# Masked copies of the 128x128 inverses: from VectorE to GpSimd from the third level on

## The chip, the cores and the metric

The kernel runs on one core of a Trainium2 chip. The metric is the device time of one launch in microseconds (us); lower is better. A core has TensorE (PE in the views, with its weight loads as PEld), VectorE (DVE), ScalarE (ACT), GpSimd (POOL), and SyncE (SP), which here only starts transfers. Each engine works through its own instructions in the order in which they are written, and engines meet only at semaphores.

## The reference, cut to what matters

The program is two transformer-like blocks, one after the other, over 1024 tokens of width 1024. The change sits in the gated delta rule of the second block. Per head and chunk of tokens it solves a unit lower triangular system, and then a short recurrence runs over the chunks:

```python
m_low = jnp.where(strict, jnp.einsum('nbhid,nbhjd->nbhij', kb, kc) * decay, 0.0)
lhs = m_low + jnp.eye(CHUNK, dtype=jnp.float32)
sol = lax.linalg.triangular_solve(lhs, rhs, left_side=True, lower=True, unit_diagonal=True)
u, w = sol[..., :dv], sol[..., dv:]
...
v_new = u_i - jnp.einsum('bhcd,bhde->bhce', w_i, S)
o = jnp.einsum('bhcd,bhde->bhce', qd_i, S) + jnp.einsum('bhij,bhje->bhie', attn_i, v_new)
S = S * gl_i[..., None, None] + jnp.einsum('bhcd,bhce->bhde', kd_i, v_new)
```

The kernel uses chunks of 128 tokens in place of 64, which gives the same output, and computes the inverse of `lhs` instead of solving. The inverse is built by doubling: if the inverses of the diagonal blocks of size s are known, those of size 2s follow from the part of the matrix that lies between two neighbouring blocks. With 128 rows there are seven levels, 0 to 6.

## The kernel before, in words

There are 4 heads and 8 chunks, so 32 matrices of 128x128. Four of them (two chunks, two heads) lie side by side in one tile of 128x512 and are worked on as one group, so there are 8 groups, b = 0 to 7. Four lanes share them: lane 0 does groups 0 and 2, lane 1 does 4 and 6, lane 2 does 1 and 3, lane 3 does 5 and 7 (`LANES`). A lane has four work tiles (`WB[n]`), all called wb in the views: `Mm` (the matrix), `Tm`, `Yy` and `Ml` (its masked copy). The running inverse of a group is in `Z`.

Each engine has a generator per lane (`prep_pe`, `prep_act`, `prep_dve`), and each `yield` ends a step. One group takes 16 steps: four of preparation, and then two for each level l = 1 to 6. `delta_steps` runs the same numbered steps s = 0 to 50 on TensorE, ScalarE and VectorE. In a step it takes the lanes in the order 0, 1, 2, 3; lane n starts at s = 4n; from s = 20 on a piece of the recurrence over the chunks (`chunk_pe` and its like) follows the lanes. So lane 0 has its first group at s = 0 to 15 and its second at s = 16 to 31, lane 1 has them four steps later, lane 2 eight and lane 3 twelve.

The work of a level l of one group:

- First step of the level. TensorE multiplies with the masked copy (L2959, four products of 128x128, "the y product" below, semaphore kind `pp_y`), and for l > 1 transposes `Z` (L2964). ScalarE copies both results from PSUM (L2992, L2996). VectorE, once the y product has read `Ml`, writes the masked copy for the next level into it (`lmask(l + 1)`, L3035, kind `pp_l`); it has one `Ml` per lane.
- Second step of the level. TensorE multiplies again (L2971), and VectorE subtracts the result from `Z` (L3056, kind `pp_z`), which the next level's y product needs.

The masked copy is `Ml = Mm * lev[l]`, 128x512 numbers, with a 0/1 mask of 128x128 repeated four times. Copies for levels 0 and 1 are made during the preparation.

The preparation has a product of decays (L2929, named bg), from which VectorE makes two tiles (L3015, L3017); ScalarE takes exponentials of them (L2979, L2982, L2985); TensorE multiplies keys with keys and queries (L2942, L2945), and VectorE scales (L3023).

What sets the order is only the order in which the code is written, engine by engine, and the waits. A wait is for a count of a semaphore that several kinds share: all of TensorE's signals of this stage (`prep_pe` in the order listings) count in TensorE's order. GpSimd does nothing in this stage; its last work lies some 1400 us earlier.

Of the kernel before, what the change touches and what calls it, by code (L numbers as in the profile page):

```python
# [195 lines left out]
class Signals:  # L196
# [18 lines left out]
    def give(self, kind, *which):  # L215
        return self.count(kind, which, 1)
# [112 lines left out]
def build(nc, A, out, scr, spill, bsc):  # L329
    from contextlib import ExitStack  # L330
    ctx = ExitStack()
    with ctx:
        sig = Signals(lambda kind: ctx.enter_context(nc.semaphore(kind)))
        give, land = sig.give, sig.land
# [449 lines left out]
        def s5_pool(pool):  # L784
            pool.wait_ge("xn_lo", 7)
            pool.wait_ge("bsc")
            pool.e.memset(Mk, 0.0).then_inc(*give("s5_mzero"))
# [1101 lines left out]
        def sb_pool(pool):  # L1889


            def mask(t, ds, *signal):
                pool.e.affine_select(out=t[:, ds], in_=t[:, ds], pattern=[[1, 128]], compare_op=ALU.is_gt,
                                     fill=0.0, base=0, channel_multiplier=-1).then_inc(*give(*signal))

            for h in range(4):
                units = SBU[h]
                n = len(units)
                for i in range(n + 3):
                    if i < n and units[i]["ds"]:  # L1900
                        u = units[i]
                        pool.wait_ge("sb_sp", u["n"])
                        mask(sbwk[u["n"] % 5][1], u["ds"], "sb_masked", u["n"])
                    if 0 <= i - 2 < n and units[i - 2]["ds"]:
                        u = units[i - 2]
                        pool.wait_ge("sb_w", u["n"])
                        mask(sbwk[u["n"] % 5][0], u["ds"], "sb_y", u["n"])
# [162 lines left out]
        FH, FSG, _, FUV = ffn_tiles(y_at + TB, False)  # L2070
# [283 lines left out]
        lev = mem("lev", y_at + 9728, [128, 896])  # L2354
# [564 lines left out]
        v3 = lambda z: z.rearrange("p (n c) -> p n c", n=4)  # L2919
        i3 = ident.unsqueeze(1).to_broadcast([128, 4, 128])  # L2920

        def prep_pe(pe, ring, b, wb):
            Mm, Tm, Yy, Ml = wb
            Zb = Z[:, b, :]
            yield
            ps = bank.take(pe, ring, f"bg{b}", ("pp_ex", b))
            pe.wait_ge("pp_lb", b)
            for n in range(4):
                ins = pe.e.matmul(ps[:, sl[n]], Ml[:, sl[n]], upper, start=True, stop=True)  # L2929
            ins.then_inc(*give("pp_bg", b))  # L2930
            yield
            ba = bank.take(pe, ring, f"ba{b}", ("pp_m", b))
            bq = bank.take(pe, ring, f"bq{b}", ("pp_at", b))
            for n, (c, h) in enumerate(PREP[b]):
                cc = slice(128 * c, 128 * c + 128)
                kx, qx = FT[h][1], FT[h][0]
                pe.wait_ge("unit", 4 + h)
                pe.wait_ge("unit", h)
                if h < 2:
                    pe.wait_ge(f"lane{2 * h}", "unpark")  # L2940
                    pe.wait_ge(f"lane{2 * h + 1}", "unpark")
                ka = pe.e.matmul(ba[:, sl[n]], kx[:, cc], kx[:, cc], start=True, stop=True)  # L2942
                if n == 3:
                    ka.then_inc(*give("pp_a", b))
                kq = pe.e.matmul(bq[:, sl[n]], kx[:, cc], qx[:, cc], start=True, stop=True)  # L2945
            kq.then_inc(*give("pp_q", b))
            yield
            ps = bank.take(pe, ring, f"bt{b}", ("pp_z", b, 0))
            pe.wait_ge("pp_l", b, 0)
            for n in range(4):  # L2950
                ins = pe.e.transpose(ps[:, sl[n]], Ml[:, sl[n]], ident)
            ins.then_inc(*give("pp_t", b))
            yield
            for l in range(1, 7):
                ps = bank.take(pe, ring, f"b1{b}{l}", ("pp_ye", b, l))
                pe.wait_ge("pp_l", b, l)
                pe.wait_ge("pp_z", b, l - 1)
                for n in range(4):
                    ins = pe.e.matmul(ps[:, sl[n]], Ml[:, sl[n]], Zb[:, sl[n]], start=True, stop=True)  # L2959
                ins.then_inc(*give("pp_y", b, l))  # L2960
                if l > 1:
                    ps = bank.take(pe, ring, f"b3{b}{l}", ("pp_tm", b, l))
                    for n in range(4):
                        ins = pe.e.transpose(ps[:, sl[n]], Zb[:, sl[n]], ident)  # L2964
                    ins.then_inc(*give("pp_zT", b, l))
                yield
                ps = bank.take(pe, ring, f"b2{b}{l}", ("pp_z", b, l))
                pe.wait_ge("pp_ye", b, l)
                pe.wait_ge("pp_tm", b, l) if l > 1 else pe.wait_ge("pp_t1", b)
                for n in range(4):  # L2970
                    ins = pe.e.matmul(ps[:, sl[n]], Tm[:, sl[n]], Yy[:, sl[n]], start=True, stop=True)  # L2971
                ins.then_inc(*give("pp_tx", b, l))
                yield
# [26 lines left out]
        def prep_dve(dve, b, wb, before):  # L3000
            Mm, Tm, Yy, Ml = wb
            Zb, ATb = Z[:, b, :], AT[:, b, :]
            if before is None:
                dve.wait_ge("prod", O0 - 1)
            else:
                dve.wait_ge("pp_tx", before, 6)
            dve.wait_ge("la")
            for n, (c, h) in enumerate(PREP[b]):
                ins = dve.e.tensor_scalar(Ml[:, sl[n]], ones, la[:, c, h:h + 1], None, ALU.mult)
                ins.then_inc(*(give("pp_lb", b) if n == 3 else dve.step()))  # L3010
            yield
            bg = bank.of(f"bg{b}")
            dve.wait_ge("pp_bg", b)
            dve.wait_ge("c_mS")
            dve.e.scalar_tensor_tensor(v3(Tm), v3(bg), -1.0, mS.unsqueeze(1).to_broadcast([128, 4, 128]), ALU.mult, ALU.add).then_inc(*give("pp_d", b, 0))  # L3015
            dve.wait_ge("c_mT")
            dve.e.tensor_tensor(v3(Yy), v3(bg), mT.unsqueeze(1).to_broadcast([128, 4, 128]), ALU.add).then_inc(*give("pp_d", b, 1))  # L3017
            yield
            ba, bq = bank.of(f"ba{b}"), bank.of(f"bq{b}")
            for n, (c, h) in enumerate(PREP[b]):  # L3020
                dve.wait_ge("pp_a", b)
                dve.wait_ge("pp_e1", b, 3)
                ins = dve.e.scalar_tensor_tensor(Mm[:, sl[n]], ba[:, sl[n]], beta[:, c, h:h + 1], Tm[:, sl[n]], ALU.mult, ALU.mult)  # L3023
                ins.then_inc(*(give("pp_m", b) if n == 3 else dve.step()))
            dve.wait_ge("pp_q", b)
            dve.wait_ge("pp_e2", b, 3)
            dve.e.tensor_tensor(ATb, bq, Yy, ALU.mult).then_inc(*give("pp_at", b))
            for n, (c, h) in enumerate(PREP[b]):
                qx = FT[h][0][:, 128 * c:128 * c + 128]
                dve.wait_ge("pp_ex", b)  # L3030
                dve.e.tensor_tensor(qx, qx, Ml[:, sl[n]], ALU.mult).then_inc(*dve.step())

            def lmask(l):
                m = lev[:, 128 * l:128 * l + 128].unsqueeze(1).to_broadcast([128, 4, 128])
                dve.e.tensor_tensor(v3(Ml), v3(Mm), m, ALU.mult).then_inc(*give("pp_l", b, l))  # L3035

            dve.wait_ge(*dve.last)
            dve.wait_ge("pp_m", b)
            dve.wait_ge("c_lev")
            lmask(0)  # L3040
            yield
            dve.wait_ge("pp_l", b, 0)
            dve.e.scalar_tensor_tensor(v3(Tm), v3(Ml), -1.0, i3, ALU.mult, ALU.add).then_inc(*give("pp_t1", b))
            dve.wait_ge("pp_t", b)
            dve.e.scalar_tensor_tensor(v3(Zb), v3(bank.of(f"bt{b}")), -1.0, i3, ALU.mult, ALU.add).then_inc(*give("pp_z", b, 0))
            dve.wait_ge("pp_t1", b)
            lmask(1)
            yield
            for l in range(1, 7):
                if l < 6:  # L3050
                    dve.wait_ge("pp_y", b, l)
                    lmask(l + 1)
                yield
                dve.wait_ge("pp_tx", b, l)
                dve.wait_ge("pp_z", b, l - 1)
                dve.e.tensor_tensor(Zb, Zb, bank.of(f"b2{b}{l}"), ALU.subtract).then_inc(*give("pp_z", b, l))  # L3056
                yield

# [73 lines left out]
        def lane_of(prep, eng, n, *ring):  # L3134
            for b in LANES[n]:
                yield from prep(eng, *ring, b, WB[n])
# [362 lines left out]
        def gpsimd(pool):  # L3499
            s5_pool(pool)  # L3500
            sb_pool(pool)

        def sync(sp):
            input_sp(sp)
# [100 lines left out]
```

## Time and profile before

| | us |
|---|---|
| median of 3 runs | 3736.06 |
| lowest and highest | 3735.85, 3736.31 |
| the profiled execution: its own time | 3736.58 |
| the profiled execution: span of the trace | 3735.0 |
| TensorE busy | 3535.2 |
| VectorE busy | 1655.9 |
| ScalarE busy | 1167.6 |
| GpSimd busy | 25.1 |

Busy times come from the first part of the page. The stage of the change lies between 2626 and 2832 us of the span, a little over 5% of it. A matmul's busy time overlaps that of its neighbour, so the pitch at which groups of matmuls start says more than the sum: a y product (four products in eight records) starts 0.89 us after the one before when nothing waits.

### The profile page before, as it was taken

The page shows a single profiled execution, that of the slowest core. Times are in us where ns is not written, and L with a number is a line of the kernel's source. Part 1 is how long each engine was busy: PE and PEld are TensorE (multiplying, and loading weights), DVE is VectorE, ACT ScalarE, POOL GpSimd, SP SyncE. Part 2 cuts the span into 40 slices and gives each one's busy share as a digit, 9 for nine tenths or more (in the row PEclk, how much of TensorE's full clock was granted, in tenths as well). Part 3 has the DMA queues.
Part 4 walks back from the last instruction along what each step waited for, and adds up shares of the span by engine and source line. Part 5 has one row for each costly group of instructions (what it writes and reads, how often), then busy time and mean ns, then how long its engine had stood idle before and what let it go on. Part 6 is the DMA issues. An engine that isn't in the chain of part 4 may idle for free.

```text
span 3735.0 us, 38804 instructions
## 1 busy us (share of the span) xinstructions
PE 3535.2 (95%) x16598; PEld 2863.6 (77%) x16598; DVE 1655.9 (44%) x2033; ACT 1167.6 (31%) x1610; POOL 25.1 (1%) x69
## 2 busy tenths in 40 slices
PE   7999999998999899999999979999899899999997
PEld 5778887777766688888888858787797588888785
DVE  7444452224554344333233364444764453534354
ACT  3232213333255623111111145344343521212122
POOL 0000000000000000000000000000000000000000
PEclk9999999999999999999999989999999999999998
DMA  2213241112400121111111112121112011111111
GB/s 107 58 48 127 82 170 44 45 50 94 138 29 23 39 86 68 44 53 46 57 35 62 39 44 85 62 90 62 46 46 101 18 50 53 47 55 38 54 35 56
DMA packets 80971, 232.11 MB, mean 62 GB/s; under 512 B 12296, under 2 KB 22280, under 8 KB 80784
## 3 DMA queue, kind: packets, MB, share of 16 engines
q1 hardware_dynamic: 80800, 229.64, 18.5%
q8 instruction: 131, 2.15, 0.2%
q14 instruction: 40, 0.33, 0.0%
HBM read 201.04 MB, written 27.38 MB: 61 GB/s over the span
## 4 chain that ended last, share of the span: by engine, by line
PE 83%; DVE 8%; ACT 7%; issue 1%; DMA 1%; SPq 0%; ACTq 0%; DVEq 0%
PE PS L431 71%; PE PS L443 2%; PE PS L2959 1%; PE PS L2971 1%; PE PS L1757 1%; PE PS L1466 1%; ACT dS L1520 1%; PE PS L858 1%; PE PS L449 1%; PE PS L1779 1%; DVE xlo L465 1%; DVE dO L1584 0%; PE PS L2964 0%; DVE wlo L396 0%; ACT whi L391 0%
## 5 line engine op out<-in xcount | busy, mean ns | idle before, releaser
L431 PE MATMUL PS<-xhi,whi 128*128 128x512 f32 x3120 | 996.4, 401 | 52.3 <-DVE xlo L465 37.0
L431 PE MATMUL PS<-xlo,whi 128*128 128x512 f32 x3120 | 969.9, 392 | 0.0
L431 PE MATMUL PS<-xhi,wlo 128*128 128x512 f32 x3120 | 967.3, 391 | 0.0
L431 PEld LDWEIGHTS PS<-xhi,whi 128*128 128x128 f32 x3120 | 583.5, 190 | 198.0 <-issue 49.8
L431 PEld LDWEIGHTS PS<-xlo,whi 128*128 128x128 f32 x3120 | 590.6, 189 | 125.8
L431 PEld LDWEIGHTS PS<-xhi,wlo 128*128 128x128 f32 x3120 | 590.3, 189 | 125.5
L396 DVE TENSOR_TENSOR wlo<-raw,whi 128x1024 fp32r<-128x1024 f32 (+3 forms) x307 | 329.6, 1075 | 504.3 <-ACT whi L391 504.2
L391 ACT CAST whi<-raw 128x1024 fp32r<-128x1024 f32 (+3 forms) x307 | 284.2, 926 | 505.3 <-PE PS L431 484.8
L431 PE MATMUL PS<-fhi,whi 128*128 128x512 f32 x704 | 218.5, 392 | 8.5 <-DVE flo L465 8.5
L431 PE MATMUL PS<-flo,whi 128*128 128x512 f32 x704 | 217.9, 391 | 0.0
L431 PE MATMUL PS<-fhi,wlo 128*128 128x512 f32 x704 | 217.8, 391 | 0.0
L431 PEld LDWEIGHTS PS<-fhi,whi 128*128 128x128 f32 x704 | 132.6, 189 | 37.6 <-DVE flo L465 10.2
L431 PEld LDWEIGHTS PS<-fhi,wlo 128*128 128x128 f32 x704 | 133.0, 189 | 27.8
L431 PEld LDWEIGHTS PS<-flo,whi 128*128 128x128 f32 x704 | 132.9, 189 | 27.7
L462 ACT CAST fhi<-fuv 128x1024 fp32r<-128x1024 f32 x44 | 46.1, 1049 | 328.5 <-DVE fuv L2149 221.9
L431 PE MATMUL PS<-yhi,whi 128*128 128x512 f32 x352 | 111.4, 398 | 8.2 <-DVE ylo L465 8.2
L431 PE MATMUL PS<-ylo,whi 128*128 128x512 f32 x352 | 110.3, 395 | 0.0
L431 PE MATMUL PS<-yhi,wlo 128*128 128x512 f32 x352 | 110.2, 395 | 0.0
L2216 DVE TENSOR_SCALAR fcb<-fsg,V 128x1024 f32<-128x1024 f32 x44 | 35.7, 812 | 163.9 <-ACT fsg L2192 163.9
L2232 DVE SCALAR_TENSOR_TENSOR merged<-PS,mod,merged 128x1024 f32<-128x1024 f32 x32 | 41.1, 1284 | 149.9 <-PE PS L431 149.9
L2156 DVE TENSOR_TENSOR merged<-PS,merged 128x1024 f32<-128x1024 f32 x32 | 39.2, 1224 | 137.8 <-PE PS L431 137.8
L2192 ACT COPY fsg<-PS 128x1024 f32<-128x1024 f32 x44 | 44.6, 1015 | 174.3 <-PE PS L431 174.3
(473 smaller groups left out, 3656.2 us busy)
## 6 DMA issues: line engine op xcount, KB each, us to landing
raw<-in_w_up SPq DMA_DIRECT2D x88, 512.0 KB, 3.3
raw<-in_w_in SPq DMA_DIRECT2D x67, 512.0 KB, 3.3
adr<-in_w_ada SPq DMA_DIRECT2D x48, 512.0 KB, 4.5
raw<-in_w_gate SPq DMA_DIRECT2D x32, 512.0 KB, 3.4
raw<-in_w_down SPq DMA_DIRECT2D x32, 384.0 KB, 3.1
raw<-in_w_down SPq DMA_DIRECT2D x32, 320.0 KB, 2.9
raw<-in_w_br SPq DMA_DIRECT2D x24, 256.0 KB, 2.7
x<-in_xT SPq DMA_DIRECT2D x8, 512.0 KB, 8.3
```

The source lines that it names most:

```text
L391: act.e.copy(whis[i % RING][:, 0:kt, :], raws[i % RING][:, 0:kt, :]).then_inc(*give("w_hi", i))
L396: dve.e.tensor_tensor(wlos[i % RING][:, 0:kt, :], raws[i % RING][:, 0:kt, :], whis[i % RING][:, 0:kt, :].bitcast(F32), ALU.subtract).then_ ...
L431: ins = pe.e.matmul(ps[:, h * 512:(h + 1) * 512], w[s][:, k, :], x[:, h * 512:(h + 1) * 512], start=(at == 0 and n == 0), stop=(at == kt - ...
L443: ins = pe.e.matmul(ps[:, h * 512:(h + 1) * 512], ones, x[:, h * 512:(h + 1) * 512], start=first, stop=last)
L449: ins = pe.e.transpose(ps[:, j * 128:(j + 1) * 128], src[:, j * 128:(j + 1) * 128], ident)
L462: act.e.copy(dst, src).then_inc(*give(*signal))
L465: dve.e.tensor_tensor(dst, src, hi.bitcast(F32), ALU.subtract).then_inc(*give(*signal))
L858: ins = pe.e.matmul(o, H[m][rows, n, :], CL[m][rows, i, 1:9, :].rearrange("p a b -> p (a b)"), start=False, stop=(m == 1), skip_group_chec ...
L1466: ins = pe.e.matmul(ps[:, 64 * h:64 * h + 64], dP[u % 2][:, n, k, :], Vt[:, k0 // 128 + k, 64 * h:64 * h + 64], start=(k == 0), stop=(k == ...
L2156: dve.e.tensor_tensor(X2[:, ft, :], psum.of(j), X2[:, ft, :], ALU.add).then_inc(*give("f1_x", c, ft))
L2192: act.e.copy(GSG[v][:, FPAD:], psum.of(j)).then_inc(*give("f2_raw", v, i))
L2232: dve.e.scalar_tensor_tensor(X1[:, ft, :], psum.of(j), gt_f(ft), X1[:, ft, :], ALU.mult, ALU.add).then_inc(*give("f2_x", c, ft))
```

## The change

The masked copies for levels 2 to 6 leave VectorE (`lmask(l + 1)` for l = 1 to 5) and are made on GpSimd by a new generator, `prep_pool`. They get a semaphore of their own, `pp_lp`, and the y product waits for that one from level 2 on. GpSimd's instruction waits for the same two things: the y product of level l, and `pp_z` of level 0.

GpSimd does not run under `delta_steps` but under a loop of its own, `delta_pool`, of the same shape. A group takes 14 of its steps and not 16: four of preparation and two for each of l = 1 to 5.

```diff
             for l in range(1, 7):
                 ps = bank.take(pe, ring, f"b1{b}{l}", ("pp_ye", b, l))
-                pe.wait_ge("pp_l", b, l)
+                pe.wait_ge("pp_l", b, l) if l < 2 else pe.wait_ge("pp_lp", b, l)
                 pe.wait_ge("pp_z", b, l - 1)
...
             for l in range(1, 7):
-                if l < 6:
-                    dve.wait_ge("pp_y", b, l)
-                    lmask(l + 1)
                 yield
...
+        def prep_pool(pool, b, wb):
+
+            Mm, Tm, Yy, Ml = wb
+            for _ in range(4):
+                yield
+            for l in range(1, 6):
+                pool.wait_ge("pp_y", b, l)
+                pool.wait_ge("pp_z", b, 0)
+                m = lev[:, 128 * (l + 1):128 * (l + 1) + 128].unsqueeze(1).to_broadcast([128, 4, 128])
+                pool.e.tensor_tensor(v3(Ml), v3(Mm), m, ALU.mult).then_inc(*give("pp_lp", b, l + 1))
+                yield
+                yield
+
+        def delta_pool(pool):
+            pool.wait_ge("c_lev")
+            lanes = [lane_of(prep_pool, pool, n) for n in range(4)]
+            for s in range(44):
+                for n in range(4):
+                    if s >= 4 * n:
+                        next(lanes[n], None)
...
         def gpsimd(pool):
             s5_pool(pool)
             sb_pool(pool)
+            delta_pool(pool)
```

The `Ml` tiles of lanes 0, 1, 2 and 3 are wb_325, wb_329, wb_333 and wb_337 in the listings below.

TensorE at its steps s = 19 and 20, of the kernel before: the second group of lane 0 has its first y product, lanes 2 and 3 are still in their first groups.

```order
5801 L2971 MATMUL PS<-wb_336,wb_335 128x128 [waits prep_act]
5803 L2959 MATMUL PS<-Z_320,wb_325 128x128 [waits prep_dve]
5805 L2959 MATMUL PS<-Z_320,wb_333 128x128 [waits prep_dve]
5807 L2964 MATMUL PS<-ident_50,Z_320 128x128 x4
5808 L2959 MATMUL PS<-Z_320,wb_337 128x128 [waits prep_dve]
5810 L2964 MATMUL PS<-ident_50,Z_320 128x128 [waits prep_act]
5812 L2971 MATMUL PS<-wb_324,wb_323 128x128 [waits prep_act]
```

The same place in the changed kernel. The order is the same; the y products of lanes 2 and 3 (levels 5 and 3) now wait for GpSimd too.

```order
5801 L2971 MATMUL PS<-wb_336,wb_335 128x128 [waits prep_act]
5803 L2959 MATMUL PS<-Z_320,wb_325 128x128 [waits prep_dve]
5805 L2959 MATMUL PS<-Z_320,wb_333 128x128 [waits prep_dve,pp_lp]
5807 L2964 MATMUL PS<-ident_50,Z_320 128x128 x4
5808 L2959 MATMUL PS<-Z_320,wb_337 128x128 [waits pp_lp,prep_dve]
5810 L2964 MATMUL PS<-ident_50,Z_320 128x128 [waits prep_act]
5812 L2971 MATMUL PS<-wb_324,wb_323 128x128 [waits prep_act]
```

GpSimd of the changed kernel around the same place (nothing stands there before). Row 84 is lane 3's copy for level 2, rows 85 to 87 are GpSimd's own step 18, rows 88 to 90 its step 20, rows 91 to 93 its step 22.

```order
84 L3065 TENSOR_TENSOR wb_337<-wb_334,lev_251 128x512 [waits prep_dve,prep_pe]
85 L3065 TENSOR_TENSOR wb_325<-wb_322,lev_251 128x512 [waits prep_dve,prep_pe]
86 L3065 TENSOR_TENSOR wb_333<-wb_330,lev_251 128x512
87 L3065 TENSOR_TENSOR wb_337<-wb_334,lev_251 128x512
88 L3065 TENSOR_TENSOR wb_325<-wb_322,lev_251 128x512 [waits prep_pe]
89 L3065 TENSOR_TENSOR wb_333<-wb_330,lev_251 128x512
90 L3065 TENSOR_TENSOR wb_337<-wb_334,lev_251 128x512
91 L3065 TENSOR_TENSOR wb_325<-wb_322,lev_251 128x512 [waits prep_pe]
92 L3065 TENSOR_TENSOR wb_329<-wb_326,lev_251 128x512 [waits prep_dve,prep_pe]
93 L3065 TENSOR_TENSOR wb_337<-wb_334,lev_251 128x512
```

Row 85 waits for the y product of TensorE's row 5803, and rows 86 and 87, which are the copies that rows 5805 and 5808 wait for, stand behind it.

## Rows read from the trace of the kernel before

**Rows 1.** The page's part 1: busy time and share of each engine.
```profile
PE 3535.2 (95%) x16598; PEld 2863.6 (77%) x16598; DVE 1655.9 (44%) x2033; ACT 1167.6 (31%) x1610; POOL 25.1 (1%) x69
```

**Rows 2.** TensorE's waits, 2626 to 2832 us: waiter, releaser, us, times, longest.
```profile
PE PS L2951 <- DVE wb L3035: 5.8, 3, 4.9
PE PS L2959 <- DVE Z L3056: 4.9, 5, 1.7
PE PS L2942 <- ACT wb L2996: 4.3, 2, 2.7
PE PS L2959 <- ACT wb L2992: 4.0, 2, 2.1
```

**Rows 3.** Groups by line and shape, 2626 to 2832: count, busy us, mean ns.
```profile
L3035 DVE TENSOR_TENSOR wb<-wb,lev 128x512 f32<-128x512 f32 x56 | 37.8, 688 | 25.4 <-PE PS L2959 24.9
```

**Rows 4.** Timelines of TensorE and VectorE at step 9, then VectorE's waits, same stretch.
```profile
2651.10 1.06 PE L2929 MATMUL PS<-upper,wb 128*128 128x128 f32 x8
...
2652.42 0.69 DVE L3015 SCALAR_TENSOR_TENSOR wb<-PS,mS 128x512 f32<-128x512 f32 x1
...
DVE wb L3015 <- PE PS L2929: 1.0, 5, 0.2
```

**Rows 5.** Timelines of TensorE and VectorE at step 20: start, us, engine, line.
```profile
2706.14 1.95 PE L2959 MATMUL PS<-Z,wb 128*128 128x128 f32 x16
...
2708.37 1.06 PE L2959 MATMUL PS<-Z,wb 128*128 128x128 f32 x8
...
2707.24 0.69 DVE L3035 TENSOR_TENSOR wb<-wb,lev 128x512 f32<-128x512 f32 x1 [0.16 <-PE PS L2959]
```

**Rows 6.** The same two timelines at step 22.
```profile
2714.16 1.06 PE L2959 MATMUL PS<-Z,wb 128*128 128x128 f32 x8
...
2717.28 1.06 PE L2959 MATMUL PS<-Z,wb 128*128 128x128 f32 x8
...
2715.26 0.69 DVE L3035 TENSOR_TENSOR wb<-wb,lev 128x512 f32<-128x512 f32 x1 [1.09 <-PE PS L2959]
```

**Rows 7.** The same two timelines at step 24.
```profile
2726.17 1.95 PE L2959 MATMUL PS<-Z,wb 128*128 128x128 f32 x16
...
2727.27 0.69 DVE L3035 TENSOR_TENSOR wb<-wb,lev 128x512 f32<-128x512 f32 x1 [0.16 <-PE PS L2959]
```

**Rows 8.** The same two timelines at step 26.
```profile
2740.93 1.06 PE L2959 MATMUL PS<-Z,wb 128*128 128x128 f32 x8
...
2737.08 0.69 DVE L3035 TENSOR_TENSOR wb<-wb,lev 128x512 f32<-128x512 f32 x1 [0.64 <-PE PS L2959]
```

**Rows 9.** GpSimd: line L1893 (ns min/median/max), its groups, one timeline row.
```profile
L1893 POOL TENSOR_SCALAR_AFFINE_SELECT sbt<-sbt x64: 285/292/550, 1009.4 to 1247.9; 128x128 f32<-128x128 f32 x64
...
L787 POOL MEMSET Mk<- 128x4096 f32 x1 | 3.5, 3531 | 70.1 <-DMA bsc<-brow 70.1
L3595 POOL MEMSET const-bfloat16-1.0<- 128x1 bf16 x1 | 0.1, 101 | 0.0
...
1143.89 0.55 POOL L1893 TENSOR_SCALAR_AFFINE_SELECT sbt<-sbt 128x128 f32<-128x128 f32 x1 [3.85 <-DVE sbt L1914]
```

**Rows 10.** TensorE's timeline where it waited long: the wait stands in brackets.
```profile
2657.76 0.46 PE L2942 MATMUL PS<-FT 128*128 128x128 f32 x2 [2.71 <-ACT wb L2996]
...
2677.85 1.16 PE L2959 MATMUL PS<-Z,wb 128*128 128x128 f32 x8 [2.14 <-ACT wb L2992]
...
2761.69 1.16 PE L2959 MATMUL PS<-Z,wb 128*128 128x128 f32 x8 [1.91 <-ACT wb L2992]
```

**Rows 11.** Stretches: length, then busy us (records) of PE, PEld, DVE, ACT, POOL; then PEclk.
```profile
2658.60:2661.60 3.00, 3.00 (x16) 3.00 (x16) 1.11 (x5) 0.00 (x0) 0.00 (x0) 0.50 0.00 0
2679.00:2682.00 3.00, 3.00 (x17) 3.00 (x15) 0.69 (x1) 1.32 (x3) 0.00 (x0) 0.50 0.00 0
...
2739.40:2742.40 3.00, 3.00 (x30) 3.00 (x29) 1.50 (x5) 0.88 (x3) 0.00 (x0) 1.00 0.00 0
2761.80:2764.80 3.00, 3.00 (x26) 2.83 (x27) 0.69 (x1) 2.27 (x5) 0.00 (x0) 1.00 0.03 5
```

## The prediction

> **What bounds the kernel now.** I read the page's busy shares first: TensorE is busy 95% of the span, VectorE 44%, GpSimd 1% [rows 1]. So what counts is when TensorE stands still. The second view is the list of TensorE's waits in the stage of the change, 206 us long [rows 2]. There the largest entries are a handful of waits of some us in total each: for VectorE's L3035 (5.8), for VectorE's update of Z (4.9), and for ScalarE's copies (4.3 and 4.0). Together the four are 19.0 us, and this is all that a lighter VectorE could attack. The third view is the timelines of TensorE and VectorE: they say for each of these waits whether a masked copy of level 2 or higher stood ahead of the releaser. The reader is to see that the releaser nearly always started because of TensorE itself, a fraction of a us after the product it needed.
>
> **What leaves VectorE.** 56 masked copies of 688 ns run there now [rows 3]. 40 of them go (8 groups, 5 levels): 27.5 us of VectorE's busy time. They are worth only what TensorE waited behind them. The 5.8 us of L2951 [rows 2] is a wait for the copy of level 0, which stays on VectorE. The two waits for ScalarE follow the exponentials, which start when VectorE has made L3015 and L3017. In 5 of 7 cases L3015 itself waited for TensorE's product L2929 (the last row of [rows 4]), so no copy in front of it held it back. In one of the others, at step 9, L3015 started at 2652.42 without a wait, 1.32 us after its product began at 2651.10 [rows 4]; after the 0.89 us of that product and a hand-over of 0.2 it could have started at 2652.2. That is a gain of **0.2 us**. The waits for Z come behind updates that were themselves released by TensorE, or behind work that stays (copies of keys, weight halves). I take 0.2 us for the whole relief; its upper bound is one copy, 0.69 us, at each of the two preludes not covered by the 5, so 1.4 us, and it can't fall below nothing.
>
> **What GpSimd's order adds.** The copy for level l + 1 is wanted one level later, 9 us or more on, so in most steps GpSimd has time for three copies of a us or two. The exception comes from the 14 steps per group where the other engines have 16. From GpSimd's step 18 on, lane 0's copies for its second group stand two steps too early: each waits for a y product of TensorE's step s + 2, and the copies of lanes still in their first group, which TensorE needs in that very step s + 2, stand behind it. It lasts until all lanes are in their second group, so it touches TensorE's steps 20, 22, 24 and 26. With T for one copy on GpSimd and 0.1 us for the hand-over back to TensorE (the 0.2 of rows 4 at most):
>
> - Step 20. Lane 0's y product starts at 2706.14 and lane 2's at 2706.14 + 0.89 = 2707.03 [rows 5]. VectorE could start its copy behind lane 0's product at 2707.24, and so can GpSimd. It makes two copies before lane 2 may go on: 2707.24 + 2T + 0.1 against 2707.03, a wait of 2T + 0.31.
> - Step 22. Lane 0's product is seen at 2715.26, lane 2 wants to start at 2717.28, since lane 1's preparation lies between [rows 6]: 2T - 1.92.
> - Step 24. Here lane 1's first product of its second group comes directly before lane 3's: seen at 2727.27, wanted at 2726.17 + 0.89 = 2727.06 [rows 7]: 2T + 0.31.
> - Step 26. Seen at 2737.08, wanted at 2740.93 [rows 8]: 2T - 3.75, which is nothing below T = 1.87.
>
> The third copy in steps 20 and 22 is in time as long as T is under 1.34, the distance 2708.37 - 2707.03 [rows 5]. So the sum is 6T - 1.30 us for T between 0.96 and 1.34. Behind each wait stand the transposes, the third lane's product and the piece of the recurrence, so the whole stage shifts; I find no later wait that would swallow it, because those that follow hang on ScalarE's chain, which starts from TensorE's L2929 and shifts too.
>
> **What T is.** No multiplication on GpSimd is in the trace. Below, it is bounded by the memset: 3531 ns for 4096 columns, 101 ns for one [rows 9], so 0.84 ns a column and 0.53 us for 512, with nothing read. Above, I put twice the cost per column of the mask of 128x128, which reads one operand: (292 - 101)/128 = 1.5 ns a column, twice that for two operands is 3.0, and 1.64 us for 512. Four times the 292 ns gives 1.17 us. I take **1.25 us**: nearest to that row, which reads and writes as the copy does, with a little for the second operand, which is a small mask read four times. That makes 6 x 1.25 - 1.30 = **6.2 us**: 2.8, 0.6 and 2.8.
>
> The Trainium skill, page "GPSIMD Engine Reference", section "Performance versus the Vector engine", gives 4497 ns for an addition of two operands of 2048 columns, which would be 1.12 us for 512, an estimate, and a sum of 5.4 us. No row here shows it.
>
> **What the waits do to the clock.** After waits of 2.71 and 2.14 us TensorE's clock was granted at one half for more than 3 us [rows 10, 11]; after 1.91 us it stayed full. At one half, 16 or 17 records start in 3 us, at full 30 [rows 11]; a stretch of some 3.4 us so costs 1.6 us. The two new waits of 2.8 us are of the kind that brought it, but whether one does hangs on what lies just around it. I take one of the two, **1.6 us**; bounds 0 and 3.2.
>
> **Sum.** -0.2 + 6.2 + 1.6 = +7.6 us. On the profiled execution's own time, 3736.58, that is 3744.2; the median of the runs lies 0.5 lower, so **3743.7 us**. 0.2% of this time is 7.5 us, about what a measurement of this kernel tells from no change; the forecast stands just over it.
>
> **Rivals.**
>
> 1. *No slower stretch of the clock*: the same waits, the clock stays at 2.4 GHz. +6.0, 3742.1 us, which counts as no change. For it: 1.91 us left the clock alone [rows 10, 11]. Against: 2.14 did not. Both waits throttled give +9.2, 3745.3 us.
> 2. *GpSimd is fast (the other side)*: it makes the copy at the memset's pace, T = 0.53. Then only steps 20 and 24 wait, 1.4 us each, too short for the clock: +2.5, 3738.6 us, not slower. It decides below T = 1.0 or so, where sum and clock stay under 5 us. Against it: a mask of a quarter of the size already takes 292 ns [rows 9].
> 3. *Shared access to SBUF*: one of the 64 masks took 0.55 us and not 0.29, right as VectorE read SBUF [rows 9]. If each copy loses time so, and VectorE in turn stands behind copies, T is 2.0: steps 20 and 24 wait 4.3 each, 22 2.1, step 26 0.25, the third lanes 2 x 0.66 more; with both stretches of slow clock +15.3, 3751.4 us. Against it: in steps 20 and 24 VectorE has little left to do. The Trainium skill, page "SBUF — State Buffer", section "Who interferes with whom", says that a VectorE instruction with two SBUF inputs and a GpSimd instruction that reads SBUF exclude each other for their whole length; the 0.55 us agrees, and by that rule most of VectorE's updates of Z, whose second input is in PSUM, would not collide.
> 4. *The relief counts after all*: waits that I put down to TensorE's own chain shrink, because VectorE reaches L3015 and Z earlier everywhere. To end faster by over 0.2% it would have to take 13 of the 19.0 us [rows 2], since GpSimd's order costs 6. I see no place for it.
>
> **How the numbers follow.** The forecast (one slow stretch, T near 1.25) has 0.42, both slow 0.23, none 0.17, rival 2 0.07, rival 3 0.07, rival 4 0.04. The forecast lies on the border, so a good half of it counts as slower: slower 0.24 + 0.23 + 0.06 = 0.53, faster 0.04, no change 0.43. The range for 8 in 10 goes from T = 1.0 with no slow stretch (4.7 - 0.2 = +4.5, 3740.6) to both slow at T = 1.5 (7.7, the third lanes 2 x 0.16, 3.2, less 0.2: +11.0, 3747.1); I widen it by a us or so on each side, towards rivals 2 and 3: 3739.5 to 3748.5.
>
> **What would show it.** In the changed profile: VectorE 27 us less busy, GpSimd with 40 instructions more; TensorE's L2959 waiting for the new GpSimd line three times, about 2.8, 0.6 and 2.8 us, in steps 20, 22 and 24 (near 2707, 2720 and 2732) and almost nowhere else; a mean of 1.2 to 1.3 us for the copy; the clock at one half once more than before between 2700 and 2740. It is wrong if L2959 waits for GpSimd in other steps (then T is far off), if the waits for L3056 or ScalarE shrink by several us (rival 4), or if later waits take up the shift.

## The result and the profile after

| | before | after |
|---|---|---|
| median, us | 3737.12 (12 runs) | 3743.95 (12 runs) |
| lowest and highest, us | 3735.85, 3738.62 | 3742.51, 3747.75 |
| ratio, 95% interval | | 1.0019 [1.001, 1.0028] |
| profiled execution: own time, span, us | 3736.58, 3735.0 | 3747.68, 3746.1 |

The change makes the kernel 6.8 us slower in the medians, where +7.6 (3743.7 us) was forecast. The profiled execution of after is a rather long one: it is 11.1 us longer than that of before. Of these, 4.4 us arose ahead of the stage that was changed, and 1.3 us are won back behind it. All readings below therefore compare distances within the stage.

The page's busy times of the kernel after, as in [rows 1]:

```profile
PE 3539.8 (94%) x16598; PEld 2867.9 (77%) x16598; DVE 1645.0 (44%) x1993; ACT 1168.0 (31%) x1610; POOL 77.2 (2%) x109
```

VectorE has its 40 instructions fewer and GpSimd its 40 more. But VectorE is only 10.9 us less busy, not 27.5. The 16.6 us between are read further down.

TensorE's waits of after in the stage (waiter, releaser, us, times, longest), as in [rows 2]:

```profile
PE PS L2951 <- DVE wb L3035: 5.8, 3, 4.9
PE PS L2959 <- DVE wb L3009: 5.5, 2, 2.8
PE PS L2959 <- DVE Z L3053: 4.9, 5, 1.7
PE PS L2959 <- ACT wb L2992: 4.6, 4, 2.1
PE PS L2942 <- ACT wb L2996: 4.3, 2, 2.7
...
PE PS L2959 <- POOL wb L3065: 0.5, 1, 0.5
```

The entries for L2951, Z and L2942 are what they were. New are 5.5 us "for L3009" and 0.5 us for GpSimd's L3065. L2959 doesn't wait for L3009 in the program, so the name needs the timelines. TensorE's y products of steps 20, 22 and 24, and one of step 12, of after:

```profile
2711.32 1.06 PE L2959 MATMUL PS<-Z,wb 128*128 128x128 f32 x8
2715.05 1.13 PE L2959 MATMUL PS<-Z,wb 128*128 128x128 f32 x8 [2.67 <-DVE wb L3009]
...
2726.03 1.13 PE L2959 MATMUL PS<-Z,wb 128*128 128x128 f32 x8 [0.50 <-POOL wb L3065]
...
2738.84 1.13 PE L2959 MATMUL PS<-Z,wb 128*128 128x128 f32 x8 [2.79 <-DVE wb L3009]
...
2673.53 1.13 PE L2959 MATMUL PS<-Z,wb 128*128 128x128 f32 x8 [0.29 <-ACT wb L2992]
```

And beside them GpSimd's copies and VectorE's L3009 and L3035 (start, length, engine, line, count):

```profile
2712.46 3.71 POOL L3065 TENSOR_TENSOR wb<-wb,lev 128x512 f32<-128x512 f32 x3 [12.09 <-PE PS L2959]
...
2734.80 3.89 POOL L3065 TENSOR_TENSOR wb<-wb,lev 128x512 f32<-128x512 f32 x3 [7.68 <-DVE Z L3053]
...
2712.13 2.90 DVE L3009 TENSOR_SCALAR wb<-ones,g 128x128 f32<-128x128 f32 x4
...
2735.24 3.54 DVE L3009 TENSOR_SCALAR wb<-ones,g 128x128 f32<-128x128 f32 x4
...
2671.92 1.47 DVE L3035 TENSOR_TENSOR wb<-wb,lev 128x512 f32<-128x512 f32 x1
```

The order is the forecast one. Lane 0's product starts at 2711.32, GpSimd sees it at 2712.46, makes two copies, the second from 2713.69 to 2714.95, and 0.1 us later lane 2's product begins at 2715.05. L3009 ends at 2715.03, just behind the second copy, because it ran beside the copies. L3009 and the Z update that the product does wait for count on the same semaphore, `prep_dve` in the order listings, so one of its updates lies just ahead of the product, and the view takes that for the release. Experiment e1 shows that the wait is for GpSimd: it moves only GpSimd's order, and all three waits go. In e1 lane 2's product (2710.15, the second of a pair) even starts before L3009 does (2710.56).

GpSimd's copy (ns: minimum, median, maximum), and three of VectorE's groups: L3009 in the same form (minimum, median, maximum), then all by shape in the stage, as in [rows 3] (count, busy us, mean ns). The last row is of the kernel **before**:

```profile
L3065 POOL TENSOR_TENSOR wb<-wb,lev x40: 1257/1272/1627, 2637.9 to 2816.4; 128x512 f32<-128x512 f32 x40
```

```profile
L3009 DVE TENSOR_SCALAR wb<-ones,g x32: 273/280/1323, 2624.3 to 2763.0; 128x128 f32<-128x128 f32 x32
...
L3009 DVE TENSOR_SCALAR wb<-ones,g 128x128 f32<-128x128 f32 x28 | 18.4, 716 | 0.0
L3035 DVE TENSOR_TENSOR wb<-wb,lev 128x512 f32<-128x512 f32 x16 | 12.5, 784 | 0.3
L3053 DVE TENSOR_TENSOR Z<-Z,PS 128x512 f32<-128x512 f32 x48 | 31.8, 682 | 10.0 <-PE PS L2971 10.0
```

```profile
L3009 DVE TENSOR_SCALAR wb<-ones,g 128x128 f32<-128x128 f32 x28 | 6.1, 279 | 0.0
```

T is 1272 ns. VectorE's 28 instructions of L3009 take 716 ns on average instead of 279, 12.3 us more in all. But their median is still 280 ns: most are as short as before, and 13 are not, nearly all of which take about 1.3 us, the length of a whole copy. At step 20 the first two take 0.28 us each, before GpSimd's copy begins at 2712.46. The third runs from 2712.52 to 2713.81 beside the first copy, which ends at 2713.73, and the fourth ends 0.08 us behind the second copy. VectorE's 16 masked copies that stayed take 784 instead of 688 on average, with two of 1.47 us. L3009 and the masked copies account for 13.8 of the 16.6 us; the rest is mostly that busy time counts the overlap of neighbouring instructions once, and there are fewer neighbours now. The Z updates, whose second input is in PSUM, are still at 682 ns. Only two of them lie beside a copy here, but in e4 below 23 of 48 do, and there they take 671 to 690 ns.

So VectorE and GpSimd do get in each other's way, and it is mostly VectorE that stands. The Trainium skill, page "SBUF — State Buffer", section "Who interferes with whom", says that a VectorE instruction with two SBUF inputs contends with a GpSimd instruction that reads SBUF, that a tensor_scalar can do so when it runs in a 2-port mode, that one with at most one SBUF input outside these modes does not, and that in a 2-port mode whoever issues first has the shared ports for the whole instruction. The trace agrees for the masked copy, which has two SBUF inputs (688 became 1467 ns at most), and for the Z update (682 stayed). L3009 is a tensor_scalar and behaves as one in a 2-port mode would; whether it runs in one, no row here shows.

**Where the time went, by distance.** The stage is measured from TensorE's first L2951 to the y product near its end that waits 0.87 us for Z. It takes 174.04 us before and 181.99 after: 7.95 more. The shift of after against before, at the same instructions along the way, counted from the stage's start:

| up to | shift, us | what lies between |
|---|---|---|
| step 10 | 0.1 | nothing; the wait of L2942 is 2.71 in both |
| step 12 | 0.8 | lane 0's and 1's copies at 2671.56 beside L3035 at 2671.92, which took 1.47; pick-up of 0.29 at 2673.53 |
| step 20 | 3.6 | wait of 2.67 |
| step 22 | 4.4 | wait of 0.50 |
| step 24 | 7.4 | wait of 2.79 |
| end | 8.0 | another such 0.5 at step 28 (L3035 took 1.47 again) |

TensorE's waits for GpSimd's order are 5.96 us. The three steps of the shift at 20, 22 and 24 add up to 6.6. The rest of each wait's shift, 0.2 us, is the restart behind it. Sharing costs 1.1, and the relief is nothing that can be seen.

**The clock.** Stretches of after behind the three longest waits that were new or moved (length, then busy us and records of PE, PEld, DVE, ACT, POOL, then PEclk), as in [rows 11]:

```profile
2715.00:2718.00 3.00, 2.96 (x26) 2.99 (x27) 0.03 (x1) 1.53 (x3) 1.17 (x1) 1.00 0.00 0
...
2739.00:2742.00 3.00, 3.00 (x28) 3.00 (x28) 0.92 (x3) 1.07 (x2) 0.00 (x0) 1.00 0.02 5
...
2773.60:2776.60 3.00, 3.00 (x25) 2.83 (x26) 0.00 (x0) 2.34 (x5) 1.27 (x1) 1.00 0.02 5
```

The granted clock stayed at 2.4 GHz after both new waits of 2.7 and 2.8 us.

### The profile page after: what moved, and what is told of

The parts are those of the page before. It is cut to its first block, busy times and chain, and to the rows that moved or that the text cites. A ratio compares the mean times of both kernels' runs of the same rounds, so it can differ in the third digit from the quotient of the medians.

```text
span 3746.1 us, 38834 instructions
## 1 busy us (share of the span) xinstructions
PE 3539.8 (94%) x16598; PEld 2867.9 (77%) x16598; DVE 1645.0 (44%) x1993; ACT 1168.0 (31%) x1610; POOL 77.2 (2%) x109
## 4 chain that ended last, share of the span: by engine, by line
PE 83%; DVE 8%; ACT 7%; issue 1%; DMA 1%; SPq 0%; POOL 0%; ACTq 0%; DVEq 0%
PE PS L431 71%; PE PS L443 2%; PE PS L2959 1%; PE PS L1757 1%; PE PS L2971 1%; PE PS L1466 1%; ACT dS L1520 1%; PE PS L1779 1%; PE PS L449 1%; PE PS L858 1%; DVE xlo L465 1%; DVE dO L1584 0%; DVE wlo L396 0%; DVE dS L1576 0%; ACT whi L391 0%
```

## The experiments

Ten kernels ran, in three batches, each with runs of the kernel before on the same chip. "Stage" is the distance defined above.

### e1: GpSimd's group takes 16 steps as well

```diff
                 yield
+            yield
+            yield
...
-            for s in range(44):
+            for s in range(48):
```

> GpSimd's generator gets two empty steps per group, 16 instead of 14, so its copies stand in TensorE's order. Theory (the order of GpSimd's copies is the loss): the three waits of TensorE's y product for GpSimd, 2.67, 0.50 and 2.79 us in the changed kernel, are gone; the two small pick-ups of about 0.5 us at the level-1 copies of VectorE that stand behind a GpSimd copy stay; the time is 3738 us where the kernel before has 3737 (0 to +1.5 us). Rival A (GpSimd is the wrong engine for the copy: its 1.27 us against 0.69, whatever the order): the time stays at +5 to +7 us. Rival B (sharing SBUF with VectorE is the loss): +4 us or more, and VectorE's L3009 stays at some 0.7 us in place of 0.28.

Measured: 3737.84 against 3738.07 us, ratio 0.9995 [0.9987, 1.0004], as the theory expected. Stage 178.18 us, against 181.99 of after and 174.04 of before. There is no wait for L3065 and none of L2959 for L3009 any more; TensorE's waits of e1 and the place at step 21:

```profile
PE PS L2929 <- DVE wb L3009: 0.6, 1, 0.6
...
2714.56 1.13 PE L2929 MATMUL PS<-upper,wb 128*128 128x128 f32 x8 [0.58 <-DVE wb L3009]
...
2710.40 3.74 POOL L3065 TENSOR_TENSOR wb<-wb,lev 128x512 f32<-128x512 f32 x3 [3.30 <-PE PS L2959]
...
2710.56 3.85 DVE L3009 TENSOR_SCALAR wb<-ones,g 128x128 f32<-128x128 f32 x4
```

The order term is shown: with the same 40 copies on the same engine, two empty steps per group take the loss away. What is left of the sharing is visible now where it really is waited for: L3009's four instructions take 3.85 us beside GpSimd's three copies, and L2929 waits 0.58. The stage of this one execution is 4.1 us longer than before's, though the medians agree. By the same reading of distances as above, sharing makes 2.7 of it: 0.5 each at steps 12, 19 and 28, behind a masked copy that took 1.5 to 1.75 us, 0.8 at L2929, and some tenths. That is more than the 1.1 in after, where the waits for GpSimd's order cover a part of it. The medians don't show these 2.7 us, and their interval reaches only to +1.5; why, stays open. Of the 4.1 us, about 1.5 is a stretch of half clock after a wait of 1.91 us, a wait which in before and in after left the clock full:

```profile
2766.60:2769.60 3.00, 3.00 (x16) 3.00 (x15) 0.00 (x0) 1.73 (x4) 1.27 (x1) 0.51 0.03 5
```

### e2: only lane 0's groups take 16 steps

```diff
+            for _ in range(2 if b in LANES[0] else 0):
+                yield
```

> Only lane 0's groups get 16 steps on GpSimd; lanes 1 to 3 keep 14. Theory: the wait at step 20 (2.67 us) and that at step 22 (0.50) go, since there lane 0's early copies stood ahead; at step 24 lane 1's early copy still stands ahead of lane 3's, so the wait of 2.8 us stays: +3 to +4 us against the kernel before. Rival (it is the engine, not the order): nothing changes, +6 to +7 us.

Measured: 3745.39 against 3738.07 us, ratio 1.002 [1.0011, 1.0029]. The waits at steps 20 and 22 are gone, and the one at step 24, which the prediction put down to lane 1's early second group, is there. TensorE's y product at step 24 of e2, and the stretch behind it:

```profile
2736.69 1.13 PE L2959 MATMUL PS<-Z,wb 128*128 128x128 f32 x8 [2.71 <-POOL wb L3065]
...
2738.00:2741.00 3.00, 3.00 (x17) 3.00 (x16) 0.82 (x3) 0.93 (x2) 0.00 (x0) 0.52 0.02 5
```

So each wait has the cause that was named, lane by lane, and here the same wait is written down under GpSimd's own line. The total was missed: 7.3 us against the 3 to 4 expected. The stage of the profiled execution is 7.3 us longer than before's as well (181.31), and the distances within it say where: 3.0 at the wait of step 24, 1.6 in the half clock behind it, and the same 2.7 for sharing as in e1. The expectation had only the first of the three.

### e3: every copy made twice, in after's order

```diff
+                pool.e.tensor_tensor(v3(Ml), v3(Mm), m, ALU.mult).then_inc(*pool.step())
+                pool.wait_ge(*pool.last)
                 pool.e.tensor_tensor(v3(Ml), v3(Mm), m, ALU.mult).then_inc(*give("pp_lp", b, l + 1))
```

> The changed kernel, with each masked copy on GpSimd made twice in a row, the second waiting for the first, so that T is about 2.6 us (same result). Theory (waits 2T + 0.31 at steps 20 and 24, 2T - 1.92 at 22, 2T - 3.75 at 26, third copies 3T - 1.03 at 20 and 3T - 3.26 at 22): 6.8, 4.5, 5.5 and 1.5 us at the four steps, 18 us in all, so +19 to +21 us against before. Rival (a fixed cost per hand-over, not the length of the copies): +7 to +9 us.

Measured: 3768.73 against 3738.07 us, ratio 1.008 [1.0065, 1.0096]; stage 206.15. TensorE's waits of e3:

```profile
PE PS L2959 <- POOL wb L3067: 12.6, 3, 6.7
...
PE PS L2959 <- issue: 5.4, 1, 5.4
...
PE PS L2929 <- DVE wb L3009: 2.7, 1, 2.7
```

The 5.4 us marked "issue" is the wait at step 20. The list names no releaser, but GpSimd's fourth instruction there, the end of lane 2's double copy, ends at 2720.69, and the product starts 0.1 us later:

```profile
2719.43 1.26 POOL L3067 TENSOR_TENSOR wb<-wb,lev 128x512 f32<-128x512 f32 x1
...
2720.79 2.05 PE L2959 MATMUL PS<-Z,wb 128*128 128x128 f32 x8 [5.40 <-issue]
```

With it TensorE waits 18.0 us for GpSimd, the sum expected. By step the waits are 5.4, 3.3, 6.7 and 2.6 where 6.8, 4.5, 5.5 and 1.5 were expected, so the match of the sum is partly luck: 1.4 and 1.2 us too little at steps 20 and 22 cancel 1.2 and 1.1 too much at steps 24 and 26. At steps 20 and 22 the terms for two copies alone give 5.5 and 3.3 us (T is 2.62), as measured. The further wait of the third lane did not come, because TensorE ran at half clock behind the first wait and so reached that product 2.70 us after lane 2's and not 1.33. At step 24 GpSimd was still busy with lane 0's copies, until 2751.03, when it could have begun lane 1's at about 2749.7.

The other 12 us of +30 are the 2.7 for L3009 and the half clock, of which only part was in the expectation (19 to 21). The granted clock of the stage is 0.91 on average where before has 0.95, which comes to about 20 us more at half clock, an estimate of 10 us of time. Before's stage first, then e3's, in the form of [rows 11]:

```profile
2628.70:2802.80 174.10, 156.74 (x1305) 152.66 (x1305) 123.06 (x266) 76.99 (x192) 0.00 (x0) 0.95 0.09 32
```

```profile
2630.80:2837.00 206.20, 165.74 (x1305) 159.06 (x1305) 120.77 (x227) 77.17 (x192) 99.96 (x78) 0.91 0.08 27
```

### e4: every copy made twice, in e1's order

The two edits together.

> Both edits together: copies in TensorE's order, each made twice (T about 2.6 us). Theory: a copy in order has a whole level of 9 us or more, three copies of 2.6 us fit in, so TensorE hardly waits for GpSimd; only the sharing of SBUF with VectorE grows: +1 to +3 us. Rival A (engine speed counts in any order): about twice what the aligned kernel loses plus 5 us or more. Rival B (sharing is the loss): +5 us or more, without waits of TensorE for GpSimd's line.

Measured: 3744.9 against 3738.07 us, ratio 1.0015 [1.0006, 1.0024]; the single times run from 3735.8 to 3746.69. TensorE never waits for GpSimd's line. What it does wait for is again L3009, at step 17 in the first place:

```profile
PE PS L2929 <- DVE wb L3009: 3.1, 2, 2.7
...
2692.30 3.90 DVE L3009 TENSOR_SCALAR wb<-ones,g 128x128 f32<-128x128 f32 x4
```

In the right order a double copy of 2.6 us is still in time; the price is in VectorE's preparation, which shares SBUF with it. The stage is 182.27 us, 8.2 more than before's, at about the same granted clock (0.96, before 0.95). The theory expected +1 to +3 and falls. Rival B, the sharing, asked for +5 or more without a wait for GpSimd's line, and this is what came. It holds for twice the copies; with single copies in the same order, e1, the median shows no loss.

### e5: e1, and L3009 made by ScalarE

```diff
+            for n, (c, h) in enumerate(PREP[b]):
+                ins = act.e.mul(Ml[:, sl[n]], ones, la[:, c, h:h + 1])
+                ins.then_inc(*(give("pp_lb", b) if n == 3 else act.step()))
...
-            for n, (c, h) in enumerate(PREP[b]):
-                ins = dve.e.tensor_scalar(Ml[:, sl[n]], ones, la[:, c, h:h + 1], None, ALU.mult)
-                ins.then_inc(*(give("pp_lb", b) if n == 3 else dve.step()))
```

> The aligned kernel, and VectorE's L3009 (ones times la, one SBUF operand, stretched from 0.28 to 0.75 us beside GpSimd's copies) is made on ScalarE instead. Theory (sharing SBUF costs the aligned kernel some 2 us through L3009 and the level-1 copy): TensorE's wait of 0.58 us at L2929 for L3009 is gone (0.9 us of the stage), the two pick-ups at the level-1 copy (0.5 each) stay, and ScalarE, which has 28 small operations more, delays nothing at that step: about 1 us less than the aligned kernel, 3737 us where before has 3738. Rival (ScalarE is the tighter engine there): its copies come later, TensorE's waits for L2992 and L2996 grow by 1 us each at steps 10, 14, 26 and 30, +2 to +4 us.

Measured: 3740.61 against 3737.78 us, ratio 1.0007 [0.9998, 1.0016]; stage 175.38, that is 2.8 less than e1's, about half of it clock. The wait for L3009 is gone. But the first group's L2929 waits longer for ScalarE than it waited before (1.11 us), ahead of where the stage begins:

```profile
2624.64 1.44 PE L2929 MATMUL PS<-upper,wb 128*128 128x128 f32 x8 [3.80 <-ACT wb L2984]
...
2625.40:2628.40 3.00, 3.00 (x16) 3.00 (x15) 1.29 (x2) 0.96 (x3) 0.00 (x0) 0.50 1.04 408
```

The second line is the stretch behind that wait: half clock. What the stage gains is lost at its door. The 1 us expected was not seen. The median lies where the rival had put it, but the rival's waits for L2992 and L2996 did not grow, and the interval takes in no change.

### e6: e1, and ScalarE's copies by VectorE where exponentials hold ScalarE

The third and fourth largest waits of [rows 2] are for ScalarE's copies L2996 and L2992, which stand behind exponentials of another lane's preparation. In those 12 levels VectorE makes the copies.

```diff
+        BY_DVE = {(LANES[n][g], l) for n in range(4) for g in range(2) for l in range(1, 7)
+                  for m in (1, 2, 3) for h in range(2)
+                  if 16 * g + 4 * n + 2 + 2 * l == 16 * h + 4 * m + 2 and n < m}
...
+                if (b, l) in BY_DVE:
+                    dve.wait_ge("pp_y", b, l)
+                    dve.wait_ge("pp_at", b)
+                    dve.e.tensor_copy(Yy, bank.of(f"b1{b}{l}")).then_inc(*give("pp_yv", b, l))
+                    if l > 1:
+                        dve.wait_ge("pp_zT", b, l)
+                        dve.wait_ge("pp_tx", b, l - 1)
+                        dve.e.tensor_copy(Tm, bank.of(f"b3{b}{l}")).then_inc(*give("pp_tv", b, l))
```

> The aligned kernel, and at the steps in which ScalarE is held by a group's exponentials (12 levels) VectorE copies TensorE's two results from PSUM in its place, using the room that GpSimd made. Theory (the relief of VectorE is worth something only where it takes over what TensorE waits for): the waits of 2.71, 2.14, 1.60 and 1.91 us for ScalarE's copies shrink to under 0.7 each, and with them the stretches of slow clock that follow: -6 to -9 us against before. Rival (the next link of the chain, the exponentials themselves and L3023 behind them, takes the waits over): -1 to -3 us.

Measured: 3726.97 against 3737.78 us, ratio 0.9972 [0.996, 0.9983]; stage 167.74. TensorE's waits of e6, where lines stand 10 further down (L2969 is the y product, L2939 the decays' product, L3023 the old L3009):

```profile
PE PS L2961 <- DVE wb L3049: 6.5, 3, 4.9
PE PS L2969 <- DVE Z L3075: 4.9, 5, 1.7
...
PE PS L2939 <- DVE wb L3023: 2.2, 2, 1.7
...
PE PS L2969 <- ACT wb L3006: 0.9, 3, 0.3
```

The waits of 2.71, 2.14, 1.59 and 1.91 us for ScalarE are gone, and what is left of that kind is 0.9. The gain of 10.8 is above the 6 to 9 expected; 6.3 of it are seen in the stage of the profiled execution, against before. The stretches of half clock that came behind the waits of 2.71 and 2.14 are gone too, though another has come at 2647.

### e7: the same copies, on the kernel before

GpSimd idle, all masks on VectorE.

> The same copies given to VectorE, but in the kernel before, with all masked copies still on VectorE and GpSimd idle. If VectorE needed the relief for this, the gain is smaller than with the masks on GpSimd by 2 us or more (-3 to -5 us against before); if its idle time of 3 to 7 us at those steps was enough anyway, the gain is the same or larger (-6 to -9 us), since nothing shares SBUF with GpSimd.

Measured: 3724.8 against 3737.78 us, ratio 0.9966 [0.9954, 0.9979]; stage 167.02. TensorE's waits of e7:

```profile
PE PS L2952 <- DVE wb L3074: 1.7, 4, 0.6
```

These four waits of at most 0.6 us are all that the masked copies cost when VectorE has to make ScalarE's copies behind them. Against e6's 2.2 for the old L3009 that is no loss. So the edit does not need the change, and the theory that a VectorE relieved of masks would be what makes it possible falls.

### e8: e6, and L3009 made by ScalarE

> The kernel with the masks on GpSimd in order, the copies on VectorE and L3009 on ScalarE: the version with the least sharing. Theory: 1 us less than the one without the last edit, -7 to -10 us against before. Rival (ScalarE tighter): the last edit costs 1 us or more.

Measured: 3721.74 against 3737.78 us, ratio 0.9958 [0.9946, 0.9971], 16.0 us less than before. It is the fastest kernel of all, and it beats before and after. The expectation was 7 to 10, and 1 us less than e6; it is 5.2 less than e6, of which the stages (162.80 against 167.74) show 4.9, some half of it clock (0.96 of full speed granted in e6's stage, 0.98 in e8's). The wait of L2939 at the start is 3.79 us, as in e5.

### e9: e8, but the first group's L3009 on VectorE

```diff
-            for n, (c, h) in enumerate(PREP[b]):
+            for n, (c, h) in enumerate(PREP[b] if b else ()):
...
+            if b == 0:
+                dve.wait_ge("prod", O0 - 1)
+                dve.wait_ge("la")
+                for n, (c, h) in enumerate(PREP[b]):
+                    ins = dve.e.tensor_scalar(Ml[:, sl[n]], ones, la[:, c, h:h + 1], None, ALU.mult)
```

> The version with masks on GpSimd in order, copies on VectorE and L3009 on ScalarE, but L3009 of the very first group back on VectorE, since ScalarE reaches it late there (TensorE waited 3.80 us for it in place of 1.11, and 1.32 less behind). Theory: 1.3 us less than without this edit: -16 to -18 us against before, some 3720 us. Rival: that wait is taken up by the next one anyway, no difference.

Measured: 3724.78 against 3738.77 us, ratio 0.996 [0.9946, 0.9974]; stage 162.57. The first wait is back at 1.11 us, which is what the edit is for, but whether the kernel gained the 1.3 us can't be told: 14.0 us less than before here, short of the 16 to 18 expected, 16.0 for e8 on another chip, and the intervals overlap.

### e10: e9, with the masked copies back on VectorE

The one comparison of the change with everything else put right, in the same batch as e9.

> The same kernel with all masked copies back on VectorE and GpSimd idle: the move alone is undone in the best version. If the move to GpSimd is worth something once VectorE has the copies to make, this one is slower by the waits that VectorE's masks put before its copies (0.60, 0.47, 0.31 and 0.31 us), +1.5 to +2.5 us against the version with GpSimd. If the sharing of SBUF (0.5 us at each of two level-1 copies, and three waits of 0.3 us for ScalarE's copy behind them) outweighs this, it is equal or faster.

Measured: 3726.74 against 3738.77 us, ratio 0.9968 [0.9955, 0.998]; stage 164.44 against e9's 162.57. TensorE's waits of e10, and then of e9 (lines as in e6; L3081 is VectorE's copy of the transposes):

```profile
PE PS L2952 <- DVE wb L3081: 1.7, 4, 0.6
```

```profile
PE PS L2969 <- ACT wb L3015: 0.9, 3, 0.3
```

The stage is 1.9 us shorter with the masks on GpSimd, and the medians differ by 2.0, both as expected. The waits explain little of it: the four that vanish are 1.7 us, but in e9 come four new ones for ScalarE's copy, 0.9 and 0.3 us together. About 1.5 us is a stretch of half clock that e10 has and e9 has not at the same instructions. First e10, then e9:

```profile
2682.40:2685.40 3.00, 3.00 (x16) 3.00 (x16) 2.24 (x4) 1.17 (x2) 0.00 (x0) 0.50 0.03 5
```

```profile
2687.00:2690.00 3.00, 2.71 (x25) 2.51 (x24) 2.49 (x3) 2.12 (x4) 2.28 (x2) 1.00 0.02 5
```

e7, with its masks on VectorE, has such a stretch at the same instructions too, and e6 and e8 have none. These are single executions, and the medians' intervals overlap. So that the move is worth 2 us here is not shown, only that it does no harm that can be seen.

## Why the prediction was right

**Relief, -0.2 us.** Right that it is next to nothing. None was seen: L2951, Z and L2942 wait as before. e7 says the same from the other side.

**GpSimd's order, +6.2 us (2.8, 0.6, 2.8 at steps 20, 22, 24).** Right by place, size and cause: 2.67, 0.50 and 2.79, in sum 5.96, nothing at step 26. T was taken as 1.25 us and is 1.27. On TensorE's path the three cost 6.6 with their restarts. The choice of T between the memset's 0.53 and the upper 1.64 was the one that mattered, and the row that it went by, an instruction that reads and writes, led close. e1 takes all of it away, e2 takes exactly lane 0's share, and e3 scales its sum to 18.0, though there the terms of the single steps are off by over 1 us each and cancel. Rival 2 (fast GpSimd) is out by the 1257 ns of the fastest copy.

**The clock, +1.6 us.** Not borne out in the profiled execution: both waits of 2.8 us left the clock full. But e2's wait of 2.71 halved it. Whether the clock falls behind such a wait differs between kernels that differ in nothing near it, so the term was a chance and no size, and one execution doesn't say what the twelve did.

**What was left out.** Rival 3 got a chance of 0.07, since in steps 20 and 24 VectorE "has little left to do". That is the step that failed, although the sum held: VectorE runs L3009, the first instructions of the next preparation, just then. They stand behind GpSimd's copies, and hence, for the most part, VectorE is 10.9 us less busy and not 27. Its price on TensorE's path was small, 1.1 us in two places in after, since L3009 is mostly needed later than it ends, and in e1, without the waits for order, 2.7 in the trace. It also took another form than the rival's: the copies did not slow down to 2.0 us; the other engine stood still. So the sum of the forecast, 7.6, came out near the 6.8 measured with a clock term that was too high by up to 1.6 and a sharing term that was missing with 1.1. The mechanism is the forecast one, but that the total is so close is partly luck: these two errors have opposite signs.

**What would show it.** The prediction asked for L2959 waiting "for the new GpSimd line three times". The list of waits has it once; the other two stand under L3009, which ended at the same moment. A reader who goes by the list alone would call the forecast wrong.

## What to carry to other kernels

An instruction that is moved to an idle engine takes its place in that engine's own order, and this order has to follow the consumer's: count the steps of the new loop against the old ones, since two steps too few cost 6 us here and two empty steps took them back. Off the bounding engine's path a lighter VectorE is worth nothing by itself (e1: no difference); the gains came from the waits of the bounding engine that were taken away by name (e6 and e7: 11 and 13 us, e8: 16). A wait listed for an instruction that the waiter doesn't use is a hint to look at what else ended then.

## What the runs showed of the hardware

- A multiplication on GpSimd of 128x512 fp32 with a mask of 128x128 repeated four times takes 1272 ns, with 1257 at least and 1627 at most; VectorE takes 688 [rows 3].
- A VectorE instruction from SBUF to SBUF can stand for the length of GpSimd's copy: of L3009 13 instructions in after took mostly about 1.3 us and the others 0.28, on average 716 ns and in e1 751 (279 before); a masked copy 688, and up to 1467. The Z update, with an input from PSUM, did not change (682; in e4 at most 690).
- The length of a wait does not tell alone whether TensorE's clock falls to 1.2 GHz behind it. A wait of 1.91 us left it at 2.4 in before and after and halved it in e1; 2.67 and 2.79 left it in after, 2.71 halved it in e2 (0.52 in the stretch behind it).
